# Index products in units 3 and 4, token projection in float32r parts, unrolled page loops, V pages on x: one change to a hybrid decoder step

## The reference, cut to what matters

```python
q, k, v, qi, ki, wi = jnp.split(x @ w_in, A_SPLIT_POINTS, axis=-1)
ki = layer_norm(ki, idx_g, idx_b)
...
s = jnp.einsum('bqhe,bse->bqhs', qi, idx_keys)                    # 8 index heads of 64
score = jnp.einsum('bqhs,bqh->bqs', jax.nn.relu(s), wi) * IDX_SCALE
_, idx = lax.top_k(score, topk)          # 128 of 512 (prompt), 256 of 1025 (samples)
k_sel, v_sel = gather_kv(idx)            # samples: from 8 pages of 128 keys each, in HBM
logits = jnp.einsum('bqgrd,bqkgd->bqgrk', qg, k_sel) * ATTN_SCALE + bias
out = jnp.einsum('bqgrk,bqkgd->bqgrd', softmax(logits), v_sel)
```

## Time and profile before

| | us |
|---|---|
| median of 3 runs (lowest, highest) | 1253.24 (1251.89, 1255.35) |
| the profiled execution | 1253.29 |
| its span in the profile | 1251.6 |
| PE busy | 1200.9 (96%) |
| DVE, ACT, POOL busy | 708.9, 475.0, 82.2 |

### The profile page before, as it was taken

The page is one execution under the profiler, slowest core; times in us unless marked ns, Lnnn a source line. Parts: engine busy times, 40 slices in busy tenths (PEclk is TensorE's granted clock), DMA queues, the critical chain, the costliest instruction groups (busy, mean ns, idle before and its releaser), DMA issues.

```text
span 1251.6 us, 25585 instructions
## 1 busy us (share of the span) xinstructions
PE 1200.9 (96%) x9582; PEld 1105.5 (88%) x9582; DVE 708.9 (57%) x1456; ACT 475.0 (38%) x872; POOL 82.2 (7%) x118
## 2 busy tenths in 40 slices
PE   8999979999999999999999999899999999999995
PEld 4958735589899999999999988698999999999994
DVE  2288989857943342443447866778533433433477
ACT  2342127744531331332334566634422322312332
POOL 4334300100012000000000000000000000000000
PEclk9999989999999999999999999999999999999998
DMA  6698472043222222232223221141222322222222
GB/s 204 184 277 264 132 245 67 2 153 118 68 68 101 84 89 96 84 101 84 100 85 118 67 74 43 45 147 38 72 97 84 101 85 96 89 84 100 84 85 69
DMA packets 61958, 131.00 MB, mean 105 GB/s; under 512 B 7819, under 2 KB 34603, under 8 KB 61755
## 3 DMA queue, kind: packets, MB, share of 16 engines
q1 hardware_dynamic: 47899, 115.16, 28.3%
q10 hardware_dynamic: 10624, 8.26, 2.2%
q0 software_dynamic: 3360, 6.56, 1.7%
HBM read 125.41 MB, written 9.79 MB: 108 GB/s over the span
## 4 chain that ended last, share of the span: by engine, by line
PE 73%; DVE 12%; issue 6%; POOLq 3%; ACT 2%; POOL 2%; SPq 1%; DMA 1%; DVEq 0%; ACTq 0%
PE PS L605 56%; PE PS L635 7%; PE PS L1020 3%; PE PS L780 2%; PE PS L793 2%; PE PS L807 2%; DVE YA L1640 2%; SPq L395 1%; DVE YA L1627 1%; POOLq L386 1%; DVE RSTD L1632 1%; POOL IK L408 1%; POOLq L406 1%; DMA KVX<-cacheV 1%; DVE X L1646 1%
## 5 line engine op out<-in xcount | busy, mean ns | idle before, releaser
L1483 DVE TENSOR_TENSOR WLO<-WRAW,WHI 128x1024 fp32r<-128x1024 f32 x118 | 145.3, 1231 | 321.3 <-ACT WHI L1082 321.3
L1082 ACT ACTIVATE WHI<-WRAW 128x1024 fp32r<-128x1024 f32 x126 | 133.4, 1059 | 387.9 <-PE PS L605 358.9
L605 PE MATMUL PS<-XH,WHI 128*128 128x260 f32 x1184 | 241.3, 285 | 0.9 <-DVE XL L1808 0.7
L605 PE MATMUL PS<-XH,WLO 128*128 128x260 f32 x1184 | 239.2, 284 | 0.0
L605 PE MATMUL PS<-XL,WHI 128*128 128x260 f32 x1184 | 238.7, 283 | 0.0
L605 PE MATMUL PS<-HH,WHI 128*128 128x260 f32 x944 | 191.2, 284 | 0.2 <-DVE HL L1507 0.2
L605 PE MATMUL PS<-HH,WLO 128*128 128x260 f32 x944 | 190.2, 283 | 0.0
L605 PE MATMUL PS<-HL,WHI 128*128 128x260 f32 x944 | 189.9, 283 | 0.0
L605 PEld LDWEIGHTS PS<-XH,WHI 128*128 128x128 f32 x1184 | 182.8, 189 | 6.4 <-issue 5.4
L605 PEld LDWEIGHTS PS<-XH,WLO 128*128 128x128 f32 x1184 | 183.2, 189 | 0.0
L605 PEld LDWEIGHTS PS<-XL,WHI 128*128 128x128 f32 x1184 | 182.6, 189 | 0.0
(11 more groups left out here) (293 smaller groups left out, 1857.6 us busy)
## 6 DMA issues: line engine op xcount, KB each, us to landing
WRAW<-wall SPq DMA_DIRECT2D x168, 512.0 KB, 3.3
bias_skewed<-bias_seq SPq DMA_DIRECT2D x4, 1280.0 KB, 18.8
X<-xT SPq DMA_DIRECT2D x4, 520.0 KB, 6.7
X<-xT SPq DMA_DIRECT2D x1, 2080.0 KB, 11.6
yT<-X SPq DMA_DIRECT2D x8, 260.0 KB
KVB<-cacheK SPq DMA_DIRECT2D x16, 128.0 KB, 3.0
KVX<-cacheK SPq DMA_DIRECT2D x16, 128.0 KB, 2.6
KVB<-cacheK POOLq DMA_DIRECT2D x16, 128.0 KB, 7.0
```

Of the source, the lines that this page charges most:

```text
L605: mm = pe.matmul(PS[:, 2 * slot + g, 0:TG], w[:, slot, k, :], x[:, k, TG * g:TG * g + TG], start=(k == 0 and w is WHI and x is hi), stop=( ...
L1082: nc.scalar.activation(WHI[:, slot], WRAW[:, slot], ACT.Copy).then_inc(hi_done, 1)
L1483: V.tensor_tensor(WLO[:, slot], WRAW[:, slot], WHI[:, slot].bitcast(F32), ALU.subtract).then_inc(lo_dve, 1)
```

## The change

1. **Token projection in parts.** Instead of 40 float32 products there are 120 in float32r: `XH`·`WNH`, `XL`·`WNH`, `XH`·`WNL`. ACT makes `WNH` and DVE `WNL` in four pieces, between the pieces of `XH` and `XL`.
2. **Index products** stand in units 3 and 4 (12 each, 3 before every second k-tile) in the order head pair, tile, head. The samples' scores and sums stand in unit 5 (k-tiles 2 and 4). The digits stand in the slots 1 to 4, 6 to 9, 11 to 13 (before 2 to 9, 12 to 14; slot 0 is the start of unit 6, two slots a unit).
3. **DVE's rounds** are laid out anew: 9 before the digits, 12 halves with the digits and tie steps, then 5, 6, 1 and 5 rounds, and in the attention steps two halves (steps 0 to 3) and three (steps 4 to 11).
4. **Page loops are written out** on POOL and for SP's index pages. On SP the weights of units 2 and 3 stand among the index pages; the 32 page numbers are read behind the weights of units 10 to 13, two samples each.
5. **V pages on x.** `KVR` is four tiles, each on one half of `XH` or `XL`. V samples 8 and 10 lie on the halves that unit 13 is done with after its fourth k-tile; a semaphore `x_used` lets them start there.
6. **Bias.** ACT copies `BT0` (in SBUF) to columns 384 to 512 of `BT`; `load_bias(1)` loads 1024 KB instead of 2048 and is issued behind the evictions of the turned probabilities, of which the small one (`PNEW`) now comes first, with a wait of its own on PE.

```diff
-            for k in range(KT):
-                if k % 2 == 0:
-                    pe.wait_ge(x_in[k // 2], 32)
+            for q in range(4):
+                pe.wait_ge(nat_hi, q + 1)
                 for t in range(5):
-                    mm = pe.matmul(PS[0:m, t, 0:NATW], X32[:, k, t * P:t * P + m], WN[:, k, :],
+                    for k in (2 * q, 2 * q + 1):
+                        natural(t, k, XH, WNH, start=(k == 0))
+                pe.wait_ge(nat_lo, q + 1)
+                for t in range(5):
+                    for k in (2 * q, 2 * q + 1):
+                        natural(t, k, XL, WNH)
+                        mm = natural(t, k, XH, WNL, stop=(k == KT - 1))
...
-            items = [(t, h) for t in range(1, QT) for h in range(IDXH)]
+            items = [(t, h + e) for h in range(0, IDXH, 2) for t in range(1, QT) for e in range(2)]
...
-                if u == 5:
-                    between = {k: (lambda k=k: index_scores(3 * k, 3 * k + 3))
-                               for k in range(KT)}
-                elif u == 6:
-                    between = {2: sample_sums}
+                if u in (3, 4):
+                    n = 12 * (u - 3)
+                    between = {k: (lambda n=n + 3 * k // 2: index_scores(n, n + 3))
+                               for k in range(0, KT, 2)}
+                elif u == 5:
+                    between = {2: sample_scores, 4: sample_sums}
...
-SLOT_OF = (2, 3, 4, 5, 6, 7, 8, 9, 12, 13, 14)
+SLOT_OF = (1, 2, 3, 4, 6, 7, 8, 9, 11, 12, 13)
...
-            prompt_rounds(10)
-            low_part(7, 1)
+            low_part(6, 0)
+            prompt_rounds(9)
...
-                prompt_rounds(1)
+                prompt_halves(2 if r == 4 else 1)
...
-                    prompt_rounds(8)
-                elif i >= 2:
-                    prompt_halves(1)
+                    prompt_rounds(5)
+                else:
+                    prompt_halves(3 if i >= 4 else 2)
...
-            for n in (6, 7):
-                with pool.Fori(0, NPG) as pg:
+            for n in (6, 7):
+                for pg in range(NPG):
                     load_page(pool, n, pg)
...
-            numbers = page_numbers(sp, 0, (12,) + V_LATE)
             early(POOL_LO[0] // 2, 1)
             sp.wait_ge(toe_skew, 16 * 4)
             sp.wait_ge(is_relu, 3 * IDXH)
             sp.wait_ge(ds_mm, 3)
             sp.dma_start(BT0[:], bskew[:, :, 127 + 384:127 + 512]).then_inc(toe_in[0], 16)
-            with sp.Fori(POOL_LO[0] // 2 + 1, POOL_LO[1] // 2) as i:
-                for s in range(2):
-                    sp.wait_ge(lo_pool, i * 2 + (s - 1 - POOL_LO[0]))
-                    load_unit(i * 2 + s, s)
+            for u in range(POOL_LO[0] + 2, POOL_LO[1]):
+                sp.wait_ge(lo_pool, u - 1 - POOL_LO[0])
+                load_unit(u, u % 2)
+                some = late[2 * (u - POOL_LO[0] - 2):][:2]
+                numbers.update(page_numbers(sp, 0, some))
...
+        def load_first_values(eng, q, numbers):
+
+            eng.wait_ge(x_used, 1)
+            for n in V_HALF:
+                load_sample(eng, q, n, numbers)
...
+            act.wait_ge(kv_used, DB)
+            act.wait_ge(toe_in[0], 16)
+            nc.scalar.activation(BT[:, :, 384:512], BT0[:], ACT.Copy).then_inc(bt_copy, 1)
```

122 lines of the change are left out of this document (79 added, 43 removed).

## The result

The changed kernel takes 1258.92 us (median of 5 runs, 1258.58 to 1261.79) against 1253.24 us before (5 runs): a ratio of 1.0046, with an interval of 1.0031 to 1.006. The forecast was 1247.7 us, faster, with a range of 1239.5 to 1255. Both the side and the range were wrong.

A forecast was written before the change was run, and what follows sets the result against it. PE, busy 96% of the span, was taken as the whole program's clock, with DVE equally the bound in the attention. Terms -6.5 - 1.3 - 11.7 + 14 = -5.5 took 1253.2 to 1247.7 us, range 1239.5 to 1255.

The forecast's parts named there:

- In these steps DVE is as much the bound as PE: Attention, 189 to 232 us, kernel before: DVE busy 39.65 of 43 us beside PE's 39.69.
- Projection, -6.5: Token projection at the start: 120 float32r products at 0.15 us each, ending at 25.9 instead of 32.4 us.
- Index products, 0: Index products, scores and sums: same PE work wherever they stand, so no change, within 1 us either way.
- Waits up to T, -1.3: Unit 0 to T, the end of the samples' logits: waits and slow clock fall from 7.8 to 6.5 us.
- the copies move the other way: Ahead of unit 9: bias copies issued from 79.3 us, 3.4 later; unit 10's weights in at 110 after 30 us of traffic.
- V pages, -11.7: Between the samples' logits and the attention: earlier V pages let the attention start after 25.3 us instead of 37.0.
- Rounds in the attention, +14: Attention steps: 22 more halves at 0.75 us are 16.5 us, some 2.4 of it swallowed by DVE's free time.
- Behind the attention, 0: Units 14 to 167 stay as they are, so nothing was added to the sum.
- Weights as late as before: Rival: weights of units 9 and 10 land as late as before, a 9.4 us wait, total 1252 us; chance 0.1.
- The clock falls in the attention: Rival: PE's clock drops in attention steps; four slow steps eat the gain, eight give 1260 us; chance 0.08.
- The lock between DVE and POOL: Short DVE operations stall during POOL's low parts: nothing added, a hit costs PE up to 2 us; no chance given.

The follow-up runs named there:

- e5: Changed kernel with bias copies ahead of unit 8's weights, 11 halves of DVE's rounds and then 6 more moved out of the attention; 1240.79 us.
- e1: Changed kernel with the four bias copies on SP ahead of the load of unit 8's weights instead of behind it; 1253.92 us.
- e6: Kernel before with only the token projection in float32r parts, nothing else of the change; 1256.09 us, ratio 1.0017 to the kernel before.
- e9: Changed kernel with the token projection in float32 again, all else as changed; 1266.37 us, ratio 1.0109 to the kernel before.
- e3: Changed kernel with bias copies ahead of unit 8's weights and 11 halves of DVE's rounds moved out of the attention; 1243.21 us.
- e2: Changed kernel with only DVE's list altered: 11 halves of rounds moved out of the attention, bias copies still late; 1250.91 us.
- e4: Changed kernel with the attention's 32 halves left out, so it computes less; 1241.23 us in one run.
- e10: Changed kernel with POOL's page loops as loops again, SP's still written out; 1261.45 us.
- e7: Changed kernel with V pages of samples 0 and 2 late again and DVE's rounds where they stood before the change; 1249.06 us.

## Why the prediction was wrong, point by point

Two steps failed. The prediction asked, of the loads behind the bias copies, only for unit 10's, and put the wait ahead of T at 4 us; the load that PE waited for was unit 9's, 5.2 us and 1.65 of slow clock. And it took DVE as a bound in the attention alone, so that it let some of the moved rounds vanish there and saw no cost of DVE's waits ahead of it; the experiments showed that DVE's list from the first round to tile 3's mask sets the time of unit 14. By stage the traces miss the forecast by 2.0, 3.8, 2.2, 2.9 and 2.8 us, 13.7 together.

*Bound.* "In these steps DVE is as much the bound as PE" was right and not followed up. The prediction then summed PE's stages one after another, as if each ended by itself. The Trainium skill, "Perfetto Trace Analysis", section "Optimization Strategy", advises for kernels with several regimes to look at the gaps on the engine that binds, within the regime. The traces agree: of DVE's idle time between first round and mask the kernel before had 15.8 us and the changed kernel 30.5, and that difference of 14.6, less the 8.7 by which the rounds began sooner and with 2.2 less busy time, is the mask's 3.8 us delay.

*Projection, -6.5: -4.5 in the trace.* The pace was right (0.15 a product, the last rows start 0.15 apart) and the start was not: the products ran 0.27 apart until 11.9 us, almost twice the later 0.15, which over 4.2 us is 1.9 of the 2.0 us that are missing. It is the lower clock. The 1.00 that a view prints for that stretch is no measurement: the trace's record of the granted clock begins only at 11.89 us, just where the pace becomes 0.15. In e5, e1 and e6 record and pace change together at 10.8, 12.7 and 13.3 us. The ratio is also that of the rows at 115 us, where the record has the lower level: matmuls of 260 columns 0.22 apart instead of 0.12. The kernel before shows it too: its float32 products start 0.55 apart to 10.2 us and 0.28 to 0.37 behind it. The prediction had priced all 120 products at the full clock. What the stage is worth in the end was wrong altogether: nothing in e6, 3.3 in the trace of e9 and 7.4 by its median.

*Index products, 0.* They were costed by PE's work alone. Their value, as far as these traces show it, is in when DVE's rounds start and in how PE's clock goes through them: in the changed kernel the clock stays at 1.00 there, in e6, with the old order, it falls to 0.57. This term should have read: rounds 8.7 us sooner, 3.0 of it the projection's by e9. No run undoes the index products alone, so their share is what is left over and not a measurement.

*Waits up to T, -1.3: +2.5.* POOL's part came out as predicted: its pages are done at 58.3 and 77.1 instead of 66 and 90, and unit 8's low part waits for ACT. The weights of unit 10 landed at 116.9, as late as before (116.3) and not at 110, and cost nothing, since PE was late itself. Those of unit 9, named in half a sentence, landed at 110.0 and cost 5.2 and 1.65 of slow clock. The step that failed is "the copies move the other way": the 30 us of traffic were summed to unit 10, and who stood first in the queue behind the copies was not asked. T came at 146.7 instead of near 141.

*V pages, -11.7: -9.5*, the attention at T + 27.5 instead of T + 25.3. PE's second group of values ran without a wait; the first waited 1.6 us.

*Rounds in the attention, +14: +16.9.* The size of a half was right (0.75 taken; 0.73 busy and the gaps). That 2.4 us of them would vanish in DVE's free time was too much: from the attention's first step to the one that waits for the mask it took 58.56 us instead of 43.21, 15.4 of the 16.5 that the halves sum to. The step behind the mask took 4.89 instead of 3.31, at a clock of 0.65. Behind it the attention is as long as before. In the changed kernel and then in the kernel before:

```profile
174.15:232.71 58.56, 41.67 (x280) 24.35 (x277) 54.39 (x187) 32.29 (x92) 0.00 (x0) 0.97 0.14 37
232.71:237.60 4.89, 4.89 (x24) 2.66 (x25) 3.29 (x13) 1.01 (x2) 0.00 (x0) 0.65 0.01 3
```
```profile
185.68:228.89 43.21, 39.90 (x280) 23.68 (x277) 38.92 (x154) 31.84 (x90) 0.00 (x0) 1.00 0.19 50
228.89:232.20 3.31, 3.31 (x25) 1.85 (x25) 2.34 (x10) 1.15 (x4) 0.00 (x0) 1.00 0.00 0
```

*Behind the attention, 0: +2.8*, by the clock in the second layer. Nothing in the sum or the rivals had it.

*Rivals.* "Weights as late as before", 1252, was the nearest in kind; it got 0.1, and it took the wait for unit 10's. "The clock falls in the attention", 1260, has nearly the right total by luck: the clock did fall behind the mask, for 1.6 us and not for eight steps. The lock between DVE and POOL, to which the prediction gave nothing, hit twice, 1.97 us at 98.3 and 1.30 at 119.2 on an operation of 0.16, each time while POOL's low part ran; the kernel before had 2.20 and 2.32. The Trainium skill, "SBUF — State Buffer", section "SBUF: two separate sides", calls this an exclusive lock of the shared port pair, and the rows agree; e3 shows another, of 1.74. That the two keep some 2 us of distance, as the prediction said, did not hold.

The sentence that should have changed the side was there: "What hid these rounds before was the wait for V pages, and the same change takes that cover away." It was given a price, +14, but not the question that follows from it: where else is DVE idle, and can the rounds go there? The changed kernel had 8.75 us of such time at one digit. That isn't a gain of the change, but it says that the sum of stages had little slack to hide a late weight load: in e1 T came 7.3 us sooner than in the changed kernel and unit 14 6.0 sooner.

## What to carry to other kernels

Where one engine has a long list of fixed work with holes in it, keep a ledger for that engine: when its list begins, how long it is idle, when it ends. Price every edit by what it does to these, whichever engine it touches; work that filled a wait must find another hole before the wait is taken away. When loads are put in another order, name the first transfer behind each moved one in its queue and who waits for it. And a stage that gets shorter can lose its gain to the clock of the stage behind it, if a wait appears there that wasn't there.

## What the runs showed of the hardware

PE's clock fell in places that no edit touched. In the second layer's attention the same matmuls behind the same pauses of 0.54 and 1.44 us ran at 1.00 in the kernel before (16 matmuls in 2.05 us), at 0.50 in the changed kernel, e1, e2 and e4 (3.78 us in each), and went from one level to the other in e3 (3.33 us). The wait for tile 3's mask is the second such place: it was 2.20 us in the changed kernel, e1 and e10, and the clock fell behind it in the first two and stayed at 1.00 in e10, where the next step took 3.30 us instead of 4.90. The rest of the span behind the attention was 985.0 and 984.9 us in two kernels, 986.3 to 986.5 in three and 987.8 to 988.0 in the others. The Trainium skill, "TensorE: Matmul & The Clock Gate", Part 1, says that the gate's watching runs freely and isn't aligned with the kernel; these rows fit that, and don't prove it. By that reading it is where in time a pause falls, and not only how long it is, that decides these 1.6 and 2.8 us; what is shown is that the pauses' lengths don't, and that differences of that size between two kernels of this program need not come from the stages that an edit touched.

A small load behind large transfers in the same queue waits for them to land. In the twelve traces in which weights were issued before the copies had landed (all but e6), the weights issued next on SP landed 1.2 to 1.7 us behind the last of the four copies, and in e7 2.2; apart from one page each in e1 and e4, nothing that SP issued behind the copies landed before their last one. Transfers that POOL and ACT issued later did: in the changed kernel their pages of 128 KB, issued between 86 and 98 us, took 7.9 to 8.6 us, while SP's, issued from 95.4 to 98.7, took 12.3 to 14.2 and unit 9's weights 18.6. The DMA engines were full meanwhile (share 1.01 in 94 to 110), so the copies set when the queue is free, and the order in the queue who pays for it. With the copies at 82.4 there had been room before them, a share of 0.57 in 69 to 82; with the copies at 69.5 it was 0.96.

What stays open: what the index products and the halved bias load are worth by themselves; why the other runs of e9 are up to 5 us above the profiled one; what sets the moment at which the clock falls; and whether the clock fell in every run of e6.
